# Waits around the norms of two transformer blocks on one core: extra zeroing matmuls, another order and earlier splits in making h, and one table for exp and ln in the gates

## The reference, cut to what matters

```python
# first block
h = rmsnorm(x, mix_pre_w) * (1 + sc_m) + sh_m
y = hybrid_mixer(h, ...)                 # gated convolution beside gated linear attention, then w_out
x = x + g_m * rmsnorm(y, mix_post_w)     # norm of y, then ...
h = rmsnorm(x, ffn_pre_w) * (1 + sc_f) + sh_f    # ... norm of the new x
y = conv_ffn(h, w_up, ffn_conv_w, w_down)
x = x + g_f * rmsnorm(y, ffn_post_w)
# second block
h = rms_norm(x, norm1_w) * (1.0 + scale1) + shift1
# pooling branch, and stick-breaking attention:
#   z = q.k / sqrt(Dh);  a = exp(log_sigmoid(z) + suffix sum of (log_sigmoid(z) - z)), masked
x = x + gate1 * (merged @ w_o)
h2 = rms_norm(x, norm2_w) * (1.0 + scale2) + shift2
x = x + gate2 * (square(relu(h2 @ w_ff1)) @ w_ff2)
```

## Time and profile before

| | |
|---|---|
| median of three runs | 2565.06 us |
| lowest and highest | 2564.28 and 2569.33 us |
| the profiled execution: its own time | 2570.12 us |
| the profiled execution: its span | 2568.8 us |
| mean granted TensorE clock | 0.986 of full speed |
| PE busy | 2487.7 us, 97% |
| DVE busy | 1996.6 us, 78% |
| ACT busy | 1294.1 us, 50% |
| DMA | 652.27 MB at 254 GB/s |

### The profile page before, as it was taken

How to read it: one execution, slowest core, us unless ns; L and a number is a source line. 1 busy time by engine, 2 the same in 40 slices (tenths; PEclk the granted TensorE clock), 3 DMA queues, 4 the chain that set the end, 5 groups by cost and what they waited for, 6 DMA issues and landing times.

```text
span 2568.8 us, 38932 instructions
## 1 busy us (share of the span) xinstructions
PE 2487.7 (97%) x15593; PEld 2234.2 (87%) x15596; DVE 1996.6 (78%) x2626; ACT 1294.1 (50%) x1894; POOL 1.9 (0%) x7
## 2 busy tenths in 40 slices
PE   6799999899999999999899999999999999999999
PEld 5689999898888888889888888889998888888888
DVE  7989989878977888889875777997678756656655
ACT  5454445455554555555546456554454444444443
POOL 0000000000000000000000000000000000000000
PEclk9899999899999999999999999999999999999999
DMA  9988889666767778777466675888568755555553
GB/s 372 394 329 307 304 311 332 217 235 250 271 246 271 260 250 290 252 266 261 154 250 235 237 262 214 307 311 295 193 238 317 265 192 186 193 184 196 183 194 134
DMA packets 135590, 652.27 MB, mean 254 GB/s; under 512 B 13025, under 2 KB 56417, under 8 KB 69617
## 3 DMA queue, kind: packets, MB, share of 16 engines
q1 hardware_dynamic: 133938, 645.06, 70.1%
q0 software_dynamic: 432, 2.62, 0.3%
q10 hardware_dynamic: 1040, 2.11, 0.2%
HBM read 647.64 MB, written 2.10 MB: 253 GB/s over the span
## 4 chain that ended last, share of the span: by engine, by line
PE 78%; DVE 11%; DMA 6%; issue 3%; ACT 2%; DVEq 0%; SPq 0%; ACTq 0%
PE PM L551 41%; PE PM L552 21%; DMA raw<-in_w_in 5%; DVE WL L1163 4%; DVE raw L1170 3%; PE PM L548 3%; PE PM L549 3%; PE PM L550 3%; PE PS L548 2%; PE PS L549 2%; PE PS L550 2%; ACT WH L806 1%; DMA X<-in_x 0%; DVE D L1402 0%; DVE D L1221 0%
## 5 line engine op out<-in xcount | busy, mean ns | idle before, releaser
L806 ACT CAST WH<-raw 128x1024 fp32r<-128x1024 f32 (+1 forms) x881 | 883.1, 1010 | 1022.7 <-PE PM L552 690.3
L1163 DVE TENSOR_TENSOR WL<-raw,WH 128x1024 fp32r<-128x1024 f32 (+1 forms) x881 | 1019.4, 1173 | 461.1 <-ACT WH L806 458.2
L551 PE MATMUL PM<-H,WH 128*128 128x512 f32 x3072 | 1080.1, 396 | 3.9 <-DVE WL L1163 3.9
L552 PE MATMUL PM<-H,WL 128*128 128x256 f32 x3072 | 861.8, 281 | 0.0
L551 PEld LDWEIGHTS PM<-H,WH 128*128 128x128 f32 x3072 | 577.1, 188 | 138.9 <-issue 5.2
L552 PEld LDWEIGHTS PM<-H,WL 128*128 128x128 f32 x3072 | 581.4, 189 | 0.5 <-issue 0.5
L1170 DVE CUSTOM_DVE_ANT_0 raw<-raw,cb 128x2048 f32<-128x2048 f32 x192 | 437.0, 2284 | 2.3 <-DMA raw<-in_w_ada 1.2
L551 PE MATMUL PM<-FC,WH 128*128 128x512 f32 x1024 | 358.6, 393 | 0.0
L552 PE MATMUL PM<-FC,WL 128*128 128x256 f32 x1024 | 285.7, 279 | 0.0
L551 PEld LDWEIGHTS PM<-FC,WH 128*128 128x128 f32 x1024 | 191.9, 187 | 46.0
L548 PE MATMUL PM<-H,WH 128*128 128x256 f32 (+1 forms) x656 | 193.3, 295 | 32.6 <-DVE H L1194 28.1
(11 more groups left out here) (308 smaller groups left out, 3114.4 us busy)
## 6 DMA issues: line engine op xcount, KB each, us to landing
raw<-in_w_ff SPq DMA_DIRECT2D x128, 1024.0 KB, 4.9
raw<-in_w_in SPq DMA_DIRECT2D x112, 1024.0 KB, 6.2
raw<-in_w_mod SPq DMA_DIRECT2D x96, 1024.0 KB, 6.8
raw<-in_w_ada SPq DMA_DIRECT2D x96, 1024.0 KB, 6.0
raw<-in_w_up SPq DMA_DIRECT2D x80, 1024.0 KB, 5.0
raw<-in_w_down SPq DMA_DIRECT2D x64, 704.0 KB, 5.5
raw<-in_w_out SPq DMA_DIRECT2D x16, 1024.0 KB, 6.8
raw<-in_w_o SPq DMA_DIRECT2D x16, 1024.0 KB, 5.9
```

Of the source, the lines that this page charges most:

```text
L551: PE.matmul(bank(n)[:, :], wh, rhs, start=(kk == 0), stop=False)
L552: return PE.matmul(bank(n)[:, T:2 * T], wl, rhs[:, 0:T], start=False, stop=ends)
L806: S.copy(part(WH), w).then_inc(s_hi, 1)
L1163: V.tensor_tensor(part(WL), w, part(WH).bitcast(F32), ALU.subtract).then_inc(s_lo, 1)
```

## The change

- `clear` gets a second argument and issues that many more zeroing matmuls behind its two. They add zeros to the same accumulators. All three norms use 4 more in `clear(1)` and 6 more in `clear(0)`.
- Unit 2 of each opening is split at the end of the splits of the empty slot, ahead of that slot's `side`, `openings` and `results`, on both engines. Unit 3 is split at the norm's own slot: on ACT first of all, on DVE ahead of `mean_square` (third norm: ahead of `make_h`). In the loops the splits go from unit i + 2 in turn i to unit i + 3 in turns 1 to 12.
- In DVE's `make_h` only tile 0 is gated and added before the first `scaled`; before, it was three tiles. Gated and new-x work then runs two tiles ahead of the loop, not three.
- `load_ln` becomes a bare table load, and `load_logs` a load of the set that has both exp and ln. `load_logs` stands ahead of Abs in both gates, behind the waits of the step; `load_ln` is added ahead of the norm of the linear attention.

```diff
+            def clear(half, again):
                 for c in range(2):
                     zeros(PS[half][:, c * 512:(c + 1) * 512])
+                for _ in range(again):
+                    zeros(PS[half][:, 512:1024], start=False)
...
-                    clear(1)
+                    clear(1, 4)
                     PE.wait_ge(s_u, 1)
-                    clear(0)
+                    clear(0, 6)
...
             def load_ln():
-                S.activation(eps[:, 1:2], eps[:, 0:1], ACT.Ln, bias=eps[:, 0:1])
+                S.preload_act_table_set("natural_log")
+            def load_logs():
+                S.preload_act_table_set("natural_log_exp_and_others")
...
                     round_h(tmps[:, i % 4, :], i)
-                    if i + 2 < 16:
-                        round_unit(units[i + 2])
+                    if 0 < i < 13:
+                        round_unit(units[i + 3])
...
                         z = ZP[:, :, 0:384]
+                        load_logs()
                         step(S.activation(AL, z, ACT.Abs))
...
                     use = (AT_NORM1, AT_NORM2).index(s)
+                    round_unit(opening_of(use)[3])
                     S.wait_ge(s_ysum, 2 * use + 1)
...
                         round_unit(u)
+                if s + 1 in OPENS_AT:
+                    round_unit(opening_of(OPENS_AT.index(s + 1))[2])
                 side(s, 0)
...
-                for i in range(3):
-                    gated(i)
-                    if i:
-                        new_x(i - 1, own[0] - 1)
-                new_x(2, own[0])
+                gated(0)
+                new_x(0, own[0])
...
                 scaled(0)
-                scaled(1)
+                if y_of:
+                    gated(1)
+                    new_x(1, own[0])
+                else:
+                    scaled(1)
                 for i in range(16):
-                    if i:
-                        scaled(i + 1)
                     V.wait_ge(s_hh, 16 * (use + 1) + i + 1)
                     rest_h(tmps[:, i % 4, :], i)
-                    gated(i + 3)
-                    if i + 2 < 16:
-                        rest_unit(units[i + 2])
-                    new_x(i + 3, own[0])
+                    scaled(i + 1 if y_of else i + 2)
+                    gated(i + 2)
+                    if 0 < i < 13:
+                        rest_unit(units[i + 3])
+                    new_x(i + 2, own[0])
...
+                    rest_unit(opening_of(use)[3])
                     mean_square(use)
...
                         rest_unit(u)
+                if s + 1 in OPENS_AT:
+                    rest_unit(opening_of(OPENS_AT.index(s + 1))[2])
                 side(s, 0)
```

More of the change, by code:

```diff
@@ L174 @@
 NSLOT = len(SLOTS)
+OPENS_AT = (AT_NORM1, AT_NORM2, AT_NORM3)
 UNIT_ENDS, JOB_ENDS, DONE = {}, {}, []
@@ L580, in run_v, with zeros @@
                 mm.then_inc(s_unit, 1)
-            def zeros(b):
-                PE.matmul(b, zero.broadcast_to([128, 128]), zero.broadcast_to([128, 512]), start=True, stop=False)
-            def clear(half):
+            def zeros(b, start=True):
+                PE.matmul(b, zero.broadcast_to([128, 128]), zero.broadcast_to([128, 512]), start=start, stop=False)
+            def clear(half, again):
                 for c in range(2):
                     zeros(PS[half][:, c * 512:(c + 1) * 512])
+                for _ in range(again):
+                    zeros(PS[half][:, 512:1024], start=False)
             def start_up():
@@ L963, in gla @@
                 elif h == 63:
+                    load_ln()
                     S.wait_ge(s_gpe, PE_NORM)
@@ L1086, in scalar @@
             ins.then_inc(s_cact, 1)
+            load_ln()
             S.wait_ge(s_const, 2)
-            load_ln()
             S.wait_ge(s_sqmm, 1)
@@ L1132, in scalar @@
                 elif s == AT_NORM3:
+                    round_unit(opening_of(2)[3])
                     S.wait_ge(s_ysum, 5)
@@ L1636, in vector @@
                         taken(JOB_OF["wo", 0, 15 - j])
+                    rest_unit(opening_of(2)[3])
                     make_h(2, None)
```

## The result

| | before | after |
|---|---|---|
| median | 2565.08 us (12 runs) | 2571.43 us (12 runs) |
| lowest and highest | 2564.28 and 2569.33 us | 2568.01 and 2574.09 us |
| ratio, 95% interval | | 1.0025 [1.0017, 1.0032] |
| the profiled execution, its span | 2570.12, 2568.8 us | 2572.34, 2571.0 us |
| mean granted TensorE clock | 0.986 | 0.991 |

The changed kernel is 6.35 us slower. The two profiled executions stand only 2.2 us apart, since that of before is 5.0 us above its median and that of after 0.9 us.

What follows compares the result with a forecast made beforehand. The prediction took TensorE, busy 97% of the span, as the bound. Clock -5.5, delays +4.0, loop +9.3 and attention -4.9 summed to +2.9 us, which on the median gave 2568.0 us, range 2560 to 2573.

Steps and rivals of the forecast that it cites:

- Part 1: At the three norms, ten more zeroing matmuls keep PE's clock up except for one fall: 5.5 us gained.
- rival B: At the norms the clock falls all the same, 0.50 over the first unit at two or more: 2572.5 us, chance 0.20.
- Parts 2 to 4: Early splits and new tile order delay the three norms by 0.89, 2.69 and 0.4 us, 4.0 us together.
- Part 4: In make_h, fewer gated tiles ahead of the first `scaled` bring nothing and cost 0.14 us, twice.
- Part 5: In the openings' loop, earlier casts make two units take 6.33 us where 5.76 are needed: 9.3 us lost in all.
- Rival A: In the loop no chain forms, ACT's and DVE's turns stay a unit ahead of PE: 2558.7 us, chance 0.15.
- The sign: In the openings, PE waits for the rest of h of tiles 2 to 13, some 9 us in 18 or more waits.
- Part 6: In attention's gates, one table load instead of two in three pairs of heads: 4.9 us gained, bounds 2.6 and 5.8.
- The fear that both sets are loaded still: At attention's gates the pass loads both table sets still, so the edit does nothing: costs 4.9 us, 2573, chance 0.05.
- Rival C: Additions cost less at the second norm and one table brings the clock at both attention waits: 2563.8 us, chance 0.10.
- The step to the median: For the whole kernel, the +2.9 us sum was put on the median, 5.1 us below the profiled execution: 2568.0 us.

Runs made afterwards that it cites:

- experiment 6: The kernel before with the table edits and the further zeroing, its own order of DVE's work and no early units: 2557.07 us, ratio 0.9967.
- experiment 2: The changed kernel with the loop's splits as before and no unit split ahead of the norms: 2556.63 us, ratio 0.9964.
- experiment 1: The changed kernel with the loop alone undone, unit i + 2 split in turns 2 to 13: 2563.21 us, ratio 0.9987.
- experiment 4: The kernel before with the ten further zeroing matmuls at each norm alone: 2562.54 us, ratio 0.9987.
- experiment 5: The kernel of experiment 1 with unit 2's split moved behind `results` in the empty slot, on both engines: 2560.66 us, ratio 0.9982.
- experiment 7: The changed kernel with DVE's new_x ahead of rest_unit in each turn of the loop: 2567.43 us, ratio 1.0005.
- experiment 9: The kernel of experiment 6 with attention's table load ahead of the two waits of the gate's step: 2554.95 us, ratio 0.9957.
- experiment 8: The kernel before, unchanged, profiled once more: 2568.41 us in one execution.
- experiment 3: The kernel before with all of the change's table edits alone: 2561.04 us, ratio 0.9982.
- experiment 10: The kernel of experiment 6 with 10 and 14 more zeroing matmuls in `clear` at the first two norms: 2556.81 us, ratio 0.9964.
- experiment 11: The kernel of experiment 6 with the edits of experiment 9 and experiment 10 together: 2555.81 us, ratio 0.9958.

## Why the prediction was right, and where it was off

The forecast was 2568.0 us in a range of 2560 to 2573; measured was 2571.43 us. The time lies in the range and on the side named, but 3.4 us above the forecast. By 6.35 us it is just past the 5.1 us that the text called "the same", although the interval reaches down to 0.17%. The medians along the path from before to after: before to experiment 6 -8.6, on to experiment 2 -0.4, to experiment 1 +6.6, to the changed kernel +8.2.

| term | predicted | by PE's rows | by the runs |
|---|---|---|---|
| zeroing and tables | -10.4 | not summed | -8.6 |
| zeroing alone | -5.5 | openings -5.5 or -4.6 | -2.9 |
| tables alone | -4.9 | first to fourth pair -3.6 to -4.6 | -4.4 |
| delays, order | +4.0 | gaps +3.87 | +6.2 |
| loop | +9.3 | openings +9.5 | +8.2 |
| sum | +2.9 | | +5.8 |

The runs add up to 5.8 and not 6.35 because the series had their own medians of before, 2565.08 to 2565.68 us. By the runs zeroing and tables together were 1.8 us short of the forecast and the delays 2.2 us over it, while the loop cost 1.1 us less than forecast. That the loop's miss hid part of the other two is luck.

**Part 1, zeroing: the cost of the units right, the reason half right, the gain too large.** I took one fall of the clock in three norms. That is about what the units paid: of the eight profiles with these ten matmuls five had a cold first unit at the first norm and one at the second, none at the third, each some 1.5 us (experiment 4's fell in mid-unit). So rival B, two or more cold first units, fell. But the clock fell more often than that. At the first norm it fell in all eight profiles. In four of them (after, experiments 1, 5 and 7) the eight matmuls of `clear(0)` took the cold stretch, 2.96 to 3.33 us for them where 1.92 is warm; behind that the first unit was warm in three and still cold in experiment 7. In the other four (2, 4, 6 and 9) the zeroing ran warm and the unit cold. At the second norm the sums were cold in four (after, 1, 4 and 7) and the unit in one (5). That makes 13 falls in 24 norms. The zeroing gained partly by keeping the clock up, as at the third norm, and partly by standing where the cold stretch costs nothing, which the step did not have. Which of the two an execution gets changes, so the warm first unit of after at the first norm is partly luck.

The gain of 5.5 us was counted from an execution whose openings lost 7.0 us to the clock; two others with the old zeroing lost 6.1 (experiment 8) and 5.5 (experiment 3), 6.2 on average, and the eight with ten more lost 1.1 on average. By the rows that is 5.1 us gained. The runs give 2.9 us alone and 4.0 on top of the tables (2561.04 to 2557.07, give or take some 4). By the interval of experiment 4 the predicted 5.5 is at the very edge. Cold sums, which the step left out and which cost 1.5 us, do not explain the rest: with a wait of 2.27 us they were cold from the first in one of three profiles with the old zeroing and in one of five with ten more. Where the difference between rows and medians lies is open.

**Parts 2 to 4, delays: right to 0.13 us in the rows, short in the time.** The gaps grew 0.88, 2.74 and 0.25 us; 0.89, 2.69 and 0.4 were composed. L613 idles 4.79 us, "near 4.8". But the runs give 6.2, and one piece of the difference is shown: behind the wait of 4.79 us the sums ran cold in all three kernels that have it (after, experiments 1 and 7). Behind 2.27 us they ran cold from the first in four of ten profiles (and from their fourth matmul on in experiment 3, a gap of 13.26 us). The profiled execution of before was one of the four, so the comparison with its rows hid a cost of about 1.5 us that an execution of before carries only now and then (one of its two profiles did). What is left of the 2.2 us is within the uncertainty of these medians.

**Part 4 by itself** was priced at 0.28 us of the delays; experiment 2 against 6 shows -0.4, nothing that can be told.

**Part 5, the loop: right.** The chain is 3.19 us as composed, the pairs 6.38 to 6.40 us (6.33 to 6.43 predicted), 6.05 at the third norm (5.99 to 6.09), the losses 3.74, 3.75 and 2.01 (3.8, 3.8 and 1.7). Experiment 1 takes all of it away and experiment 7 the predicted part. Rival A, that the engines stay a unit ahead, fell with both. The sign that I named for it did not come, though: some 9 us in 18 or more waits for the rest of h. The list has 14 waits with 8.1 us, of which 3.27 are the first tiles of two norms; the 12 left hold some 4.8. The rest of the price is the matmul that restarts behind each wait (0.36 us and the next one 0.20 later, against 0.28 and 0.12) and, at the third norm, pauses too short for the list. The distance between unit starts is the measure.

**Part 6, tables: right.** One load is left, the waits are 1.32 and 3.32 us for 1.3 and 3.2 predicted, and 4.4 us are gained for 4.9. The half clock behind the second pair went too: in after the granted clock is 1.00 from 1541 to 1546 us, where it was 0.66, and it is 1.00 there in all ten profiles with the shared table. It is in experiment 4 as well, whose wait is still 2.59 us, so that part of the gain (1.7 us in the sum) is not there against every execution. The first of these rows is that stretch, the second the one behind the fourth pair, where the wait stayed and the clock is 0.80 (columns as in rows 3):
```profile
1541.00:1546.00 5.00, 5.00 (x33) 4.50 (x33) 5.00 (x5) 0.21 (x1) 0.00 (x0) 1.00 0.45 156
1596.00:1601.00 5.00, 5.00 (x26) 4.31 (x25) 2.10 (x4) 3.94 (x5) 0.00 (x0) 0.80 0.49 193
```
The two waits shrank by 1.28 and 1.13 us, so a switch of tables on the path is worth the load and nothing more. The Trainium skill, ScalarE: Activation LUTs, What ACT_TABLE_LOAD costs, gives 2.66 us for every switch to a different set; an estimate from that page would have each wait shrink by 2.66 us. The measurement differs, and it decides. The fear that both sets are loaded still did not come true. Rival C needed a cheaper second norm, and that norm's gap grew by 2.74 us, 0.05 more than composed.

**The step to the median.** The sum was made against a profiled execution 5 us above its median and then carried over unchanged. Its mean granted clock, 0.986, is the lowest that executions of before show here (0.986 to 0.991). It showed more of the very losses that the change was to remove than experiment 8 did (0.9 us more in the openings, 1.55 us more in the gap at the second norm, though 1.22 us less in the gap at the first). A gain read from one slow execution need not be there in the median.

## What to carry to other kernels

Work that is "early" on an in-order engine is only early if nothing urgent stands behind it: a cast of a weight unit put ahead of the last sums made TensorE wait 2.52 us longer for them, and one turn of lead less in a ring of four slots cost 0.6 us in every pair of units at two norms and 0.3 at the third. Count how long the chain from "slot free" to "next operand ready" is and compare it with the time of the units that it spans. Of the edits in this change two gained 8.6 us and the two that start weight units earlier lost 14.8; timing each alone found the version that is better than both kernels: zeroing and the shared table, without the new splits, and with the table load ahead of the waits, 2554.95 us, 0.43% under the kernel before. The zeroing and the table are what its median shows; the last step's 1.27 us are read from the rows. When runs scatter by more than an edit is worth, a short distance between two rows of one engine can still price it: the gates' stretch repeats within 0.13 us where the whole stage scatters by 2.7.

## What the runs showed that I had not expected

- The fall of the clock moves about, between the zeroing matmuls, the sums and the first unit. With more zeroing and the wait of 2.27 us, experiments 2, 6 and 9 had a cold first unit at the first norm and warm sums at the second, experiments 10 and 11 the reverse, experiment 5 a cold first unit at the second norm alone (4.43 us), and experiment 4 lost at both places. The kernel before had its first sums of the second norm at 1.19 us in one execution and at full clock in the other. Why a fall comes at one place and not at another is open; no run here tells it.
- More zeroing than four and six matmuls a norm bought nothing that can be told, though PE then idled only 0.38 us ahead of h at the second norm, and not 2.14.
- A bare table load waits like any other instruction behind the waits written ahead of it. Moved two lines up it cost PE nothing.
- Attention's stage took 547.26 to 549.98 us in three profiles without the shared table, and 541.89 to 544.59 in those with it whose kernels differ only at the norms. Scatter of 2.7 us within one stage is as large as several of the terms that were priced, and in those with the table all but 0.13 us of it lies outside the stretch from the first to the fourth pair.
